# Sums of squares per token of a hybrid attention layer, taken from the columns of x in place of its rows

## The chip, the cores and the metric

The kernel runs on one core of a Trainium2 chip. The metric is the device time of one execution in microseconds. The engines are TensorE (PE, its weight loads are PEld), VectorE (DVE), ScalarE (ACT), GpSimd (POOL) and SyncE (SP), which here only issues loads and stores.

## What is computed

One decoder layer on x of 512 tokens by 1024, all float32. Cut to what matters here:

```python
u = rms_norm(h, attn_pre_g)                 # x * rsqrt(mean(x*x) + 1e-6) * g, by token
proj = u @ w_in                             # 1024 -> 256 + 128 + 32 + 3*512
c_q, c_kv, k_r, moba_qkv = split(proj)      # latents (256 and 128), rotary key, q/k/v of 8 heads
mla_o = mla_attention(rms_norm(c_q), rms_norm(c_kv), k_r, ...)
moba_o = moba_attention(rope(q), rope(k), v)
h = h + rms_norm(concat(mla_o, moba_o) @ w_out, attn_post_g)
h = h + rms_norm(square(relu(rms_norm(h, mlp_pre_g) @ w_up)) @ w_down, mlp_post_g)
```

The change is in the first norm. Its sum of squares over the 1024 elements of each token gives one root per token, `rstd = (mean + eps) ** -0.5`.

## The kernel before, in words

Every large product is made in three passes from two float32r parts of each operand (`mm3`, L1325): hi x hi, hi x lo, lo x hi. ScalarE makes the hi part (`hi_part`, L574), VectorE the lo part (`lo_part`, L879; `lo_scaled`, L882, with the gain).

x comes to the core twice at the start. Its columns, `x_cols` (transposed on the host, with the gain as a 513th column), are loaded in eight pieces of 128 x 513 into `x_raw` (`first_x`, L358) and become `uT_hi` and `uT_lo`, the operands of all projections. They are not normed: the roots of the tokens are multiplied in later. Its rows are loaded into `x_sb` (L373) only for the sums of squares. The weights `w_in` come in chunks: chunks 0 and 1 row by row with the columns (`first_rows`, L361), the others as 1 MB each (`chunk`, L335; `in_chunk`, L344) into two raw buffers in turn. Each load waits until VectorE is done with the chunk two before it (`w_ready`).

Order of work at the start, on each engine:

- TensorE: 34 small products to warm up, `first_group` (L1338) for latents and rotary key of four tiles of 128 tokens in banks 0 to 3, then `half_group(1, before_queries)` (L1377, L1395) for the queries in banks 4 to 7. This group has two parts of four chunks of rows each (`part`), a part has four tiles j of 12 products. Ahead of tile j=2 of part 0 it turns the four columns of token roots into a row in bank 7 (L1400); tile j=3 then uses bank 7, once VectorE has copied it to `r_cols`. The latents' transposes (L1425) and the key group `half_group(2, before_keys)` follow.
- ScalarE: hi parts of the eight pieces (`first_hi`), hi part of chunk 2 (`in_hi(2)`), four squares of x rows with `accum_out` into `stat` (`square`, L597; L616), hi part of chunk 3, then for each tile of 128 tokens the squares of both latents and a scaled copy of the rotary key (L620).
- VectorE: lo parts of the eight pieces (`first_lo`), lo part of chunk 2 (`in_lo(2)`, L915), the copy to `r_cols` (L917), lo part of chunk 3, rotation tables times roots (L922), normed latents `cn` (L930), rotation of the rotary key, lo part of chunk 4.
- GpSimd: constants, then `rms` (L484) once for each of the four tiles of tokens, and twice more for each tile for the latents. It takes the mean in one operation on a 128x1 column of `stat`, the power -0.5 in another and, for the latents, a product with the token's root in a third; each waits for the one before it. `stat[:, norm, tile, :]` holds sum (0), mean (2) and root (3) of a norm; norm 0 is the tokens', 1 and 2 are the latents'.

The order on each engine is the order of the code in its block; engines meet only at semaphores: `sq` counts sums of squares, `rstd` roots, `proj` finished projection tiles.

Of the kernel before, what the change touches and what calls it, by code (L numbers as in the profile page):

```python
# [20 lines left out]
ALU = mybir.AluOpType  # L21
ACT = mybir.ActivationFunctionType

P = 128
EPS = 1e-6
NEG = -1e30
NOPE, ROPE, VD = 64, 32, 64
# [5 lines left out]
def build(nc, x, attn_pre_g, w_in, mla_q_norm_g, w_mla_q_up, mla_kv_norm_g, w_mla_kv_up, w_out,  # L33
          attn_post_g, mlp_pre_g, w_up, w_down, mlp_post_g, rope_table, x_cols, rope_cols, out):
    S, D = x.shape[1], x.shape[2]
    F = w_up.shape[2]
    QR, KVR = w_mla_q_up.shape[1], w_mla_kv_up.shape[1]
    NT = S // P
    ND = D // P
# [9 lines left out]
    x_v = x[0].rearrange("(t p) d -> t p d", p=P)  # L49
# [26 lines left out]
    with ExitStack() as ctx:  # L76
        def sb(name, shape, dt=F32, stack=ctx):
            return stack.enter_context(nc.sbuf_tensor(name, shape, dt))

        def sem(name):  # L80
            return ctx.enter_context(nc.semaphore(name))
# [7 lines left out]
        stat = sb("stat", [P, 6, NT, 4])  # L89
        half = stat[:, 4, 0, 1:2]  # L90
        nb = sb("nb", [P, 4, NT])
# [26 lines left out]
        with ExitStack() as start:  # L118
            x_sb = sb("x_sb", [P, NT, D], stack=start)
            junk_pre = sb("junk_pre", [P, D], BF16, stack=start)  # L120
# [5 lines left out]
        with ExitStack() as pre:  # L126
            lat_g = sb("lat_g", [P, QR + KVR], stack=pre)
            rope_sb = sb("rope_sb", [P, NT, rope_table.shape[1]], stack=pre)
            cn = sb("cn", [P, NT, QR + KVR], stack=pre)
            kr = sb("kr", [P, NT, ROPE], stack=pre)  # L130
            krr = sb("krr", [P, NT, ROPE], stack=pre)
            r_cols = sb("r_cols", [P, S], stack=pre)
            turn = sb("turn", [P, 2, S], stack=pre)
            rt1 = sb("rt1", [P, NT, HW], stack=pre)
            rt2 = sb("rt2", [P, 2, HW], stack=pre)
# [35 lines left out]

        x_in = [sem(f"x{t}_in") for t in range(NT)]
        x_cols_in = [sem(f"x_cols{k}_in") for k in range(ND)]
# [13 lines left out]
        sq = sem("sq")  # L187
# [146 lines left out]
        def _(sp):  # L334
# [37 lines left out]
            in_chunk(2)  # L372
            for t in range(NT):  # L373
                sp.dma_start(x_sb[:, t, :], x_v[t]).then_inc(x_in[t], 16)
            sp.dma_start(rope_sb[:, :, :], rope_table.rearrange("(t p) c -> p t c", p=P)).then_inc(tab_in, 16)
            sp.dma_start(lat_g[:, 0:QR], mla_q_norm_g.to_broadcast([P, QR])).then_inc(lat_in, 16)
# [90 lines left out]
        def _(pool):  # L467
# [3 lines left out]
            nc.gpsimd.memset(half, -0.5).then_inc(zeroed, 1)  # L471
            pool.wait_ge(zeroed, 3)
            nc.gpsimd.affine_select(out=ident[:, :], in_=ident[:, :], compare_op=ALU.not_equal, fill=1.0, base=0,
# [25 lines left out]

            for t in range(NT):  # L500
                rms(0, t, D, t + 1)

            for t in range(NT):
                rms(1, t, QR, NT + 2 * t + 1, by=stat[:, 0, t, 3:4])
                rms(2, t, KVR, NT + 2 * t + 2, by=stat[:, 0, t, 3:4])

# [52 lines left out]
        def _(act):  # L559
# [34 lines left out]

            squares = [0]

            def square(src, norm, t, col, scale=1.0):  # L597
                if squares[0]:
                    act.wait_ge(sq, squares[0])
                squares[0] += 1  # L600
                junk = junk_pre if norm <= 2 else junk_post if norm <= 4 else junk_down
                nc.scalar.activation(junk[:, 0:src.shape[1]], src, ACT.Square, scale=scale,  # L602
                                     accum_out=stat[:, norm, t, col:col + 1]).then_inc(sq, 1)
# [11 lines left out]
            in_hi(2)  # L615
            for t in range(NT):  # L616
                act.wait_ge(x_in[t], 16)
                square(x_sb[:, t, :], 0, t, 0)
            in_hi(3)
# [251 lines left out]
        def _(dve):  # L871
# [41 lines left out]
            for k in range(ND):  # L913
                first_lo(k)
            in_lo(2)  # L915
            dve.wait_ge(r_full, 1)
            nc.vector.tensor_copy(r_cols[:, :], ps[7][:, :]).then_inc(r_ready, 1)  # L917
# [8 lines left out]
            for t in range(NT):  # L926
                dve.wait_ge(kr_c, t + 1)
                for norm, c0, n in ((1, 0, QR), (2, QR, KVR)):
                    dve.wait_ge(rstd, NT + 2 * t + norm)
                    nc.vector.scalar_tensor_tensor(out=cn[:, t, c0:c0 + n], in0=ps[t][:, c0:c0 + n],  # L930
                                                   scalar=stat[:, norm, t, 3:4], in1=lat_g[:, c0:c0 + n],
                                                   op0=ALU.mult, op1=ALU.mult).then_inc(cn_ready, 1)
# [391 lines left out]
        def _(pe):  # L1324
# [70 lines left out]
            def before_queries(part, j):  # L1395

                if part == 0 and j == 2:
                    pe.wait_ge(rstd, NT)
                    for t in range(NT):
                        last = nc.tensor.transpose(ps[7][:, P * t:P * t + P], stat[:, 0, t, 3:4].to_broadcast([P, P]),  # L1400
                                                   ident[:, :])
                    last.then_inc(r_full, 1)
                if part == 0 and j == 3:
                    pe.wait_ge(r_ready, 1)
# [366 lines left out]
```

## Time and profile before

| | us |
|---|---|
| median of 3 runs | 562.36 (562.35 to 562.46) |
| the profiled execution | 562.25 |
| its span, first to last instruction | 560.5 |
| TensorE busy | 548.9 (98%), 2730 instructions |
| VectorE busy | 392.2 (70%), 745 |
| ScalarE busy | 293.4 (52%), 612 |
| GpSimd busy | 92.2 (16%), 152 |
| moved by DMA | 99.66 MB |

All times below are from the start of the span, which is 1.75 us shorter than the execution. The trace writes the buffers of PSUM as `bank`, without their number, and names of buffers without their numbers. A product's record covers its way through the pipeline, so records overlap: the distance between two starts is what one costs in a row of them. "Idle before" is what an engine sat idle ahead of an instruction, with what ended it.

### The profile page before, as it was taken

The numbers are of one execution on the slowest core, as the hardware profiler recorded it, in microseconds if no ns is written. First come the engines' busy times: TensorE is split into PE (matmuls) and PEld (weight loads), VectorE is DVE, ScalarE is ACT, GpSimd is POOL, SyncE is SP. The second block draws the span as 40 slices with busy tenths as digits, with TensorE's granted clock in tenths as the row PEclk, the third lists the DMA queues.
The fourth block names the chain that finished last, engine by engine and source line by source line (L and its number), as shares of the span: only waits on it lengthen the run. The fifth ranks groups of instructions, "written<-read, shape, count | busy, mean of one in ns | idle before, by whom it ended". The sixth has DMA issues, their size and how long they took to land.

```text
span 560.5 us, 7840 instructions
## 1 busy us (share of the span) xinstructions
PE 548.9 (98%) x2730; PEld 451.9 (81%) x2730; DVE 392.2 (70%) x745; ACT 293.4 (52%) x612; POOL 92.2 (16%) x152
## 2 busy tenths in 40 slices
PE   9999999999999999999999999999999999999994
PEld 8888898876656888988888888888888888888883
DVE  5359473487785366367766775779777989778897
ACT  6563172688884364463344335344465656656561
POOL 1263110355784012200000000000000001000003
PEclk9999999999999999999999999999999999999999
DMA  8933652000002940387778886787975565605403
GB/s 289 370 123 104 201 165 76 0 2 2 0 2 76 340 149 1 108 297 272 229 277 279 278 283 229 276 279 265 357 280 195 181 216 167 219 21 204 150 1 150
DMA packets 43454, 99.66 MB, mean 178 GB/s; under 512 B 3232, under 2 KB 20896, under 8 KB 40096
## 3 DMA queue, kind: packets, MB, share of 16 engines
q1 hardware_dynamic: 42992, 98.54, 51.0%
q10 hardware_dynamic: 432, 0.74, 0.4%
q8 instruction: 17, 0.28, 0.2%
q14 instruction: 13, 0.11, 0.1%
HBM read 81.44 MB, written 15.73 MB: 173 GB/s over the span
## 4 chain that ended last, share of the span: by engine, by line
PE 91%; DMA 3%; DVE 2%; POOL 2%; ACT 1%; issue 1%; ACTq 0%; DVEq 0%; POOLq 0%
PE bank L1327 28%; PE bank L1328 27%; PE bank L1329 27%; PE bank L1539 3%; PE bank L1558 3%; POOL probs L527 1%; DMA w_raw<-in_w_in 1%; DMA x_raw<-in_x_cols 1%; PE bank L1504 1%; DVE w_lo L883 1%; PE bank L1333 1%; DVE bank L1000 1%; ACT w_hi L575 1%; ACT probs L665 0%; PE bank L1463 0%
## 5 line engine op out<-in xcount | busy, mean ns | idle before, releaser
L1327 PE MATMUL bank<-uT_hi,w_hi 128*128 128x512 f32 (+1 forms) x344 | 129.3, 376 | 0.8 <-DVE w_lo L883 0.8
L1328 PE MATMUL bank<-uT_lo,w_hi 128*128 128x512 f32 (+1 forms) x344 | 128.8, 374 | 0.0
L1329 PE MATMUL bank<-uT_hi,w_lo 128*128 128x512 f32 (+1 forms) x344 | 128.7, 374 | 0.0
L1327 PE MATMUL bank<-w_hi,a_hi 128*128 128x512 f32 x224 | 87.2, 389 | 0.0
L1329 PE MATMUL bank<-w_hi,a_lo 128*128 128x512 f32 x224 | 87.2, 389 | 0.0
L1328 PE MATMUL bank<-w_lo,a_hi 128*128 128x512 f32 x224 | 87.1, 389 | 0.0
L883 DVE SCALAR_TENSOR_TENSOR w_lo<-w_raw,g_up,w_hi 128x256 fp32r<-128x256 f32 x128 | 52.1, 480 | 48.4 <-ACT w_hi L575 48.4
L575 ACT ACTIVATE w_hi<-w_raw,g_up 128x256 fp32r<-128x256 f32 x128 | 53.0, 496 | 45.6 <-PE bank L1329 24.8
L1327 PEld LDWEIGHTS bank<-uT_hi,w_hi 128*128 128x128 f32 x344 | 64.7, 188 | 12.9 <-issue 1.1
L1328 PEld LDWEIGHTS bank<-uT_lo,w_hi 128*128 128x128 f32 x344 | 64.8, 188 | 11.5
L1329 PEld LDWEIGHTS bank<-uT_hi,w_lo 128*128 128x128 f32 x344 | 64.7, 188 | 11.4
L575 ACT ACTIVATE w_hi<-w_raw 128x1024 fp32r<-128x1024 f32 (+2 forms) x49 | 46.4, 996 | 52.4 <-PE bank L1329 48.8
L880 DVE TENSOR_TENSOR w_lo<-w_raw,w_hi 128x1024 fp32r<-128x1024 f32 (+2 forms) x45 | 51.4, 1185 | 21.5 <-ACT w_hi L575 21.5
L527 POOL TENSOR_TENSOR probs<-probs,rs 128x512 f32<-128x512 f32 (+3 forms) x64 | 44.1, 720 | 50.9 <-DVE rs L1020 44.9
L1327 PEld LDWEIGHTS bank<-w_hi,a_hi 128*128 128x128 f32 x224 | 42.0, 188 | 9.2 <-issue 0.4
L1329 PEld LDWEIGHTS bank<-w_hi,a_lo 128*128 128x128 f32 x224 | 42.0, 188 | 8.8
L1328 PEld LDWEIGHTS bank<-w_lo,a_hi 128*128 128x128 f32 x224 | 42.0, 188 | 8.6
L822 ACT ACTIVATE act_sb<-relu 128x512 f32 (+1 forms) x32 | 20.0, 624 | 51.1 <-DVE relu L1186 51.1
L551 POOL TENSOR_TENSOR relu<-relu,post_g 128x512 f32<-128x512 f32 x2 | 2.7, 1394 | 230.9 <-ACT junk_down L602 230.9
L665 ACT ACTIVATE probs<-bank,nb 128x512 f32<-128x512 f32 (+3 forms) x64 | 33.2, 524 | 13.9 <-DVE nb L1000 13.4
L1208 DVE TENSOR_TENSOR stage<-stage 128x512 f32<-128x512 f32 x56 | 38.7, 691 | 1.5
L1000 DVE CUSTOM_DVE_ANT_0 bank<-bank,mask 128x512 f32<-128x512 f32 (+3 forms) x64 | 30.0, 515 | 12.4 <-PE bank L1329 6.2
(161 smaller groups left out, 871.3 us busy)
## 6 DMA issues: line engine op xcount, KB each, us to landing
stage<-in_w_down SPq DMA_DIRECT2D x17, 1024.0 KB, 4.9
w_raw<-in_w_up SPq DMA_DIRECT2D x16, 1024.0 KB, 8.4
pair_sums<-stage SPq DMA_DIRECT2D x13, 1024.0 KB, 9.9
w_raw<-in_w_down SPq DMA_DIRECT2D x10, 1024.0 KB, 6.7
w_raw<-pair_sums SPq DMA_DIRECT2D x10, 1024.0 KB, 4.8
w_raw<-in_w_in SPq DMA_DIRECT2D x6, 1024.0 KB, 7.5
w_raw<-in_w_out SPq DMA_DIRECT2D x4, 1024.0 KB, 4.8
stage<-pair_sums SPq DMA_DIRECT2D x3, 1024.0 KB, 4.8
```

What stands on the lines that cost most here:

```text
L527: nc.gpsimd.tensor_tensor(pr, pr, rs[:, i % 4, t:t + 1].to_broadcast([P, P * (t + 1)]), ALU.mult).then_inc(s_norm, 1)
L575: return nc.scalar.activation(out, whole, ACT.Copy, scale=scale)
L665: nc.scalar.activation(probs[i % 4][:, p_off(t):p_off(t) + n], ps[b][:, c:c + n], ACT.Exp, bias=nb[:, i % 4, t:t + 1], scale=-1.0, accum_o ...
L822: nc.scalar.activation(act_sb[:, bass.ds(i * 4 + tile, 1), :], relu[:, tile % 2:tile % 2 + 1, :], ACT.Square).then_inc(a_ready, 1)
L880: return nc.vector.tensor_tensor(out, whole, hi.bitcast(F32), ALU.subtract)
L883: return nc.vector.scalar_tensor_tensor(out=out, in0=whole, scalar=scale, in1=hi.bitcast(F32), op0=ALU.mult, op1=ALU.subtract)
L1000: nc.vector.tensor_tensor_reduce(out=s, in0=s, in1=mask[:, TOP - P * (t + 1):], scale=-SCALE[i], scalar=-NEG, op0=ALU.add, op1=ALU.min, ac ...
L1208: nc.vector.tensor_tensor(total, a, b, ALU.subtract).then_inc(stage_sums, 1)
L1327: nc.tensor.matmul(out, lh, rh, start=start, stop=False)
L1328: nc.tensor.matmul(out, lh, rl, start=False, stop=False)
L1329: return nc.tensor.matmul(out, ll, rh, start=False, stop=stop)
L1539: last = nc.tensor.transpose(ps[b][:, c + P * (t - k):c + P * (t - k) + P], probs[i % 4][:, p_off(t) + P * k:p_off(t) + P * k + P], ident[ ...
```

## The change

It takes the sums of squares from `x_raw`, the columns, in place of `x_sb`, the rows:

- ScalarE squares the eight pieces of columns into `sq_cols` (8 x 128x512 float32) where it squared the four tiles of rows.
- VectorE adds the eight into the first, seven additions of 128x512, behind the lo part of chunk 2 and ahead of the copy to `r_cols`. Each waits for its square and for the addition before it.
- TensorE makes the sums over the 128 partitions: four plain float32 products with `sq_cols` as weights (128 x 128 each) and a column of ones, one column of bank 7 each, ahead of tile j=1 of part 0. It waits for the seventh addition.
- VectorE copies the four columns from bank 7 into `stat`, GpSimd makes the four roots in one pair of operations on 128x4.
- The latents' roots are made in six operations on 128x4 once all eight of their sums are there.
- The four loads of x rows at the start go; the rotation table comes in the layout of its buffer, so that each partition's part is one piece.

```diff
-        half = stat[:, 4, 0, 1:2]
+        half, one = stat[:, 4, 0, 1:2], stat[:, 4, 1, 1:2]
...
-            x_sb = sb("x_sb", [P, NT, D], stack=start)
+            sq_cols = sb("sq_cols", [P, ND, S], stack=start)
...
             in_chunk(2)
-            for t in range(NT):
-                sp.dma_start(x_sb[:, t, :], x_v[t]).then_inc(x_in[t], 16)
-            sp.dma_start(rope_sb[:, :, :], rope_table.rearrange("(t p) c -> p t c", p=P)).then_inc(tab_in, 16)
+            sp.dma_start(rope_sb[:, :, :], rope_table).then_inc(tab_in, 16)
...
-            for t in range(NT):
-                rms(0, t, D, t + 1)
-
-            for t in range(NT):
-                rms(1, t, QR, NT + 2 * t + 1, by=stat[:, 0, t, 3:4])
-                rms(2, t, KVR, NT + 2 * t + 2, by=stat[:, 0, t, 3:4])
+            pool.wait_ge(sq, NT)
+            step(nc.gpsimd.tensor_scalar(stat[:, 0, :, 2], stat[:, 0, :, 0], 1.0 / D, EPS, ALU.mult, ALU.add))
+            nc.gpsimd.tensor_tensor(stat[:, 0, :, 3], stat[:, 0, :, 2], half.to_broadcast([P, NT]), ALU.pow).then_inc(rstd, NT)
+
+            pool.wait_ge(sq, 3 * NT)
+            for norm, n in ((1, QR), (2, KVR)):
+                last = nc.gpsimd.tensor_scalar(stat[:, norm, :, 2], stat[:, norm, :, 0], 1.0 / n, EPS, ALU.mult, ALU.add)
+            step(last)
+            for norm in (1, 2):
+                last = nc.gpsimd.tensor_tensor(stat[:, norm, :, 3], stat[:, norm, :, 2], half.to_broadcast([P, NT]), ALU.pow)
+            step(last)
+            for norm in (1, 2):
+                nc.gpsimd.tensor_tensor(stat[:, norm, :, 3], stat[:, norm, :, 3], stat[:, 0, :, 3],
+                                        ALU.mult).then_inc(rstd, NT)
...
             in_hi(2)
-            for t in range(NT):
-                act.wait_ge(x_in[t], 16)
-                square(x_sb[:, t, :], 0, t, 0)
+            for k in range(ND):
+                nc.scalar.activation(sq_cols[:, k, :], x_raw[:, k, 0:S], ACT.Square).then_inc(x_squared, 1)
             in_hi(3)
...
             in_lo(2)
+            for k in range(1, ND):
+                dve.wait_ge(x_squared, k + 1)
+                if k >= 2:
+                    dve.wait_ge(x_summed, k - 1)
+                nc.vector.tensor_tensor(sq_cols[:, 0, :], sq_cols[:, 0, :], sq_cols[:, k, :], ALU.add).then_inc(x_summed, 1)
+            dve.wait_ge(x_sums, 1)
+            nc.vector.tensor_copy(stat[:, 0, :, 0], ps[7][:, 0:NT]).then_inc(sq, NT)
             dve.wait_ge(r_full, 1)
...
-                    dve.wait_ge(rstd, NT + 2 * t + norm)
+                    dve.wait_ge(rstd, NT + NT * norm)
...
             def before_queries(part, j):
 
+                if part == 0 and j == 1:
+                    pe.wait_ge(x_summed, ND - 1)
+                    for t in range(NT):
+                        last = nc.tensor.matmul(ps[7][:, t:t + 1], sq_cols[:, 0, P * t:P * t + P], one, start=True, stop=True)
+                    last.then_inc(x_sums, 1)
                 if part == 0 and j == 2:
```

TensorE, from the end of tile j=0 to the root transposes, before (L1327 to L1329 are the three passes of `mm3`, L1400 the transposes):

```order
L1327 MATMUL bank<-uT_hi,w_hi 128x512
L1328 MATMUL bank<-uT_lo,w_hi 128x512
L1329 MATMUL bank<-uT_hi,w_lo 128x512
L1400 MATMUL bank<-ident,stat 128x128 [waits rstd]
L1400 MATMUL bank<-ident,stat 128x128 x3
```

Ahead of these stand the 24 products of j=0 and j=1 without a wait but the first one's. And with the change (L1339 to L1341 are now the three passes, L1417 the transposes), from the last products of j=0 to the first of j=1:

```order
L1339 MATMUL bank<-uT_hi,w_hi 128x512
L1340 MATMUL bank<-uT_lo,w_hi 128x512
L1341 MATMUL bank<-uT_hi,w_lo 128x512
L1412 MATMUL bank<-stat,sq_cols 128x1 [waits x_summed]
L1412 MATMUL bank<-stat,sq_cols 128x1 x3
L1339 MATMUL bank<-uT_hi,w_hi 128x512
L1340 MATMUL bank<-uT_lo,w_hi 128x512
L1341 MATMUL bank<-uT_hi,w_lo 128x512
```

A wait and four products now stand between j=0 and j=1; the transposes keep their place behind j=1.

VectorE, around the lo part of chunk 2, before:

```order
L883 SCALAR_TENSOR_TENSOR w_lo<-w_raw,g_in,w_hi 128x512 [waits wh_ready]
L883 SCALAR_TENSOR_TENSOR w_lo<-w_raw,g_in,w_hi 128x512 x3
L917 COPY r_cols<-bank 128x512 [waits r_full]
L883 SCALAR_TENSOR_TENSOR w_lo<-w_raw,g_in,w_hi 128x512 [waits wh_ready]
L883 SCALAR_TENSOR_TENSOR w_lo<-w_raw,g_in,w_hi 128x512 x3
```

and with the change:

```order
L888 SCALAR_TENSOR_TENSOR w_lo<-w_raw,g_in,w_hi 128x512 [waits wh_ready]
L888 SCALAR_TENSOR_TENSOR w_lo<-w_raw,g_in,w_hi 128x512 x3
L925 TENSOR_TENSOR sq_cols<-sq_cols 128x512 [waits x_squared]
L925 TENSOR_TENSOR sq_cols<-sq_cols 128x512 [waits x_summed,x_squared] x6
L927 COPY stat<-bank 128x4 [waits x_sums]
L929 COPY r_cols<-bank 128x512 [waits r_full]
```

Seven additions and a copy that waits for TensorE stand between the lo part of chunk 2 and `r_cols`.

## Rows read from the trace of the kernel before

**Rows 1.** The profile's chain that ended last, shares of the span by engine.
```profile
PE 91%; DMA 3%; DVE 2%; POOL 2%; ACT 1%; issue 1%; ACTq 0%; DVEq 0%; POOLq 0%
```
**Rows 2.** Waits of TensorE, 0 to 250 us: in total, times, longest.
```profile
PE bank L1327 <- DVE w_lo L883: 0.8, 1, 0.8
```
**Rows 3.** The chain in order of time, 0 to 60 us: start, us, what.
```profile
10.95 7.80 DMA w_raw<-in_w_in
18.83 2.57 ACT w_hi L575 x4
21.43 2.75 DVE w_lo L883 x4
```
**Rows 4.** Timeline, TensorE: start, us, instruction, [idle before <-releaser].
```profile
24.31 0.47 PE L1327 MATMUL bank<-uT_hi,w_hi 128*128 128x512 f32 x1 [0.79 <-DVE w_lo L883]
...
27.13 0.39 PE L1327 MATMUL bank<-uT_hi,w_hi 128*128 128x512 f32 x1
...
29.85 0.60 PE L1400 MATMUL bank<-ident,stat 128*128 128x128 f32 x4
...
46.66 1.48 PE L1425 MATMUL bank<-ident,cn 128*128 128x128 f32 x12
47.97 0.60 PE L1429 MATMUL bank<-ident,krr 128*32 128x128 f32 x4
```
**Rows 5.** Timeline, ScalarE.
```profile
11.28 0.63 ACT L575 ACTIVATE uT_hi<-x_raw 128x512 fp32r<-128x512 f32 x1
...
21.30 1.04 ACT L602 ACTIVATE junk_pre<-x_sb 128x1024 bf16<-128x1024 f32 x1
...
30.14 0.45 ACT L602 ACTIVATE junk_pre<-bank,stat 128x256 bf16<-128x256 f32 x1
```
**Rows 6.** Timeline, issues of DMA by SyncE (SPq).
```profile
11.38 3.40 SPq L374 DMA_DIRECT2D x_sb<-in_x  x4
...
232.54 0.37 SPq L399 DMA_DIRECT2D stage<-in_w_down  x1
232.95 0.47 SPq L407 DMA_DIRECT2D w_raw<-in_w_up  x1
```
**Rows 7.** Timeline, GpSimd.
```profile
22.97 0.94 POOL L494 TENSOR_TENSOR stat<-stat 128x1 f32<-128x1 f32 x1
...
41.95 0.19 POOL L497 TENSOR_TENSOR stat<-stat 128x1 f32<-128x1 f32 x1
...
66.55 2.54 POOL L510 TENSOR_TENSOR rt<-rt 128x512 f32<-128x512 f32 x2 [13.86 <-DVE rt L958]
```
**Rows 8.** Issues at 10.95, 232.54, 232.95: count, KB, us to landing.
```profile
w_raw<-in_w_in SPq DMA_DIRECT2D x1, 1024.0 KB, 7.8
...
stage<-in_w_down SPq DMA_DIRECT2D x1, 1024.0 KB, 4.9
...
w_raw<-in_w_up SPq DMA_DIRECT2D x1, 1024.0 KB, 7.5
```
**Rows 9.** Timeline, VectorE.
```profile
4.40 0.44 DVE L899 TENSOR_SCALAR w_hi<-w_raw,x_raw 128x416 fp32r<-128x416 f32 x1 [4.40 <-DMA x_raw<-in_x_cols]
4.87 0.65 DVE L883 SCALAR_TENSOR_TENSOR w_lo<-w_raw,x_raw,w_hi 128x416 fp32r<-128x416 f32 x1
...
15.51 0.68 DVE L880 TENSOR_TENSOR uT_lo<-x_raw,uT_hi 128x512 fp32r<-128x512 f32 x1
...
42.64 0.22 DVE L944 TENSOR_TENSOR rt<-kr,rope_sb 128x64 f32<-128x64 f32 x1
```
**Rows 10.** Groups by shape, TensorE, 110 to 190 us: count | busy, mean ns.
```profile
L1504 PE MATMUL bank<-mkT,mqT 64*128 64x512 f32 x16 | 4.5, 641 | 0.6 <-ACT probs L665 0.6
...
L1504 PE MATMUL bank<-mkT,mqT 64*128 64x128 f32 x16 | 1.6, 270 | 0.0
```
**Rows 11.** Windows: us, busy of PE, PEld, DVE, ACT, POOL, clock, DMA share, GB/s.
```profile
553.00:555.00 2.00, 0.10 (x1) 0.00 (x0) 1.83 (x3) 0.72 (x2) 0.98 (x3) 1.00 0.00 0
...
557.00:559.00 2.00, 0.00 (x0) 0.00 (x0) 1.01 (x2) 0.00 (x0) 0.00 (x0) 0.77 0.62 238
```

More of the change, by code:

```diff
@@ L127, in build @@
             lat_g = sb("lat_g", [P, QR + KVR], stack=pre)
-            rope_sb = sb("rope_sb", [P, NT, rope_table.shape[1]], stack=pre)
+            rope_sb = sb("rope_sb", [P, NT, rope_table.shape[2]], stack=pre)
             cn = sb("cn", [P, NT, QR + KVR], stack=pre)
@@ L169, in build @@
         ps = [ctx.enter_context(nc.psum_tensor(f"bank{b}", [P, TOP], F32)) for b in range(8)]
-        x_in = [sem(f"x{t}_in") for t in range(NT)]
+        x_squared, x_summed, x_sums = sem("x_squared"), sem("x_summed"), sem("x_sums")
         x_cols_in = [sem(f"x_cols{k}_in") for k in range(ND)]
@@ L471, in _ @@
             nc.gpsimd.memset(half, -0.5).then_inc(zeroed, 1)
-            pool.wait_ge(zeroed, 3)
+            nc.gpsimd.memset(one, 1.0).then_inc(zeroed, 1)
+            pool.wait_ge(zeroed, 4)
             nc.gpsimd.affine_select(out=ident[:, :], in_=ident[:, :], compare_op=ALU.not_equal, fill=1.0, base=0,
@@ L593, in first_hi @@
                     hi_part(w_hi[w_slot(k // 4)][:, w], raw[k // 4][:, w], g_first(k)).then_inc(in_rows(k, first_h, wh_ready)[0], 1)
-            squares = [0]
+            squares = [NT]
             def square(src, norm, t, col, scale=1.0):
-                if squares[0]:
-                    act.wait_ge(sq, squares[0])
+                act.wait_ge(sq, squares[0])
                 squares[0] += 1
@@ L1757 @@
     arrays = {name: np.ascontiguousarray(inputs[name]) for name in NAMES}
-    arrays["rope_table"] = rope_constants(arrays["x"].shape[1], ROPE, 1)
+    table = rope_constants(arrays["x"].shape[1], ROPE, 1)
+    arrays["rope_table"] = np.ascontiguousarray(table.reshape(-1, P, table.shape[1]).transpose(1, 0, 2))
     arrays["x_cols"] = np.ascontiguousarray(np.concatenate([arrays["x"][0].T, arrays["attn_pre_g"][0][:, None]], axis=1))
```

## The prediction

> **What bounds the kernel now.** I read four views in this order. The chain that ended last [rows 1] puts 91% of the span on TensorE. So a change at the start is worth what it does to TensorE's instruction stream: a microsecond that another engine saves or spends there counts only if TensorE waits for it, and no later stage of the kernel waits for a load that could take a delay back.
>
> The list of waits for the first 250 us [rows 2] has one wait of TensorE between its first projection product and the attention: 0.8 us for `w_lo` of the first query chunk (chunk 2). The chain in order of time [rows 3] shows what lies behind it: the load of that chunk is issued at 10.95 and lands 7.80 us later, ScalarE makes `w_hi` from 18.83 (2.57), VectorE makes `w_lo` from 21.43 (2.75), and TensorE starts at 24.31. TensorE's own rows [rows 4] then give the timetable that the change has to fit: tile j=0 of the query group runs from 24.31 to 27.13, j=1 follows without a gap, and the four transposes of the token roots stand at 29.85, where nothing is waited for. So the only thing to gain is under 0.8 us, and everything else in this stretch is cover that can be used up.
>
> **Removed work.** ScalarE loses four squares over rows of x, 1.04 us and an accumulator read each [rows 5]; the four loads of x rows (2 MB) go, with 3.40 us of SP's issue time [rows 6]. None of it lies on the path: ScalarE's row squares start after `w_hi` of chunk 2, which is what TensorE waits for. GpSimd's roots shrink from 8 to 2 instructions for the tokens and from 24 to 6 for the latents. The last of the 24 ends at 42.14 [rows 7] while TensorE needs the latents only at 46.66 [rows 4], so this was covered by more than 3 us and is worth nothing, too. The table of rotations in another layout and the one extra constant cost nothing: the table is wanted long after it lands, and the constant is set before anything waits for GpSimd again.
>
> **Does chunk 2 land earlier without the x rows?** They are issued directly behind it [rows 6], and it takes 7.8 us where a 1 MB load from an idle queue takes 4.9 [rows 8], so they could be to blame. The nearest row says no: the load issued at 232.54 [rows 6] landed after 4.9 us although the next 1 MB load was issued 0.41 us behind it at 232.95; that second one took 7.5, as long as one that stands in line. Loads of this queue are served in line. Chunk 2 is late for what stands ahead of it, the first rows of w_in and the columns of x, which the change leaves alone. I take no gain; the bounds are none and 7.8 - 4.9 = 2.9 us.
> The Trainium skill, *DMA: Bandwidth & Descriptors*, section "Queues, rings and completion order", has the same rule: each DMA engine consumes a queue's descriptors in ring order. It speaks against the change, which takes away only loads that stand behind; these rows agree with it.
>
> **The new chain in front of j=1.** This is the term that matters. VectorE's seven adds stand behind `w_lo` of chunk 2 in its order and need each other's result. `w_lo` is done at 21.43 + 2.75 = 24.18 [rows 3]. An operation of two 128x512 fp32 tensors takes 0.68, the third row of [rows 9]; one that waits for the instruction before it on its own engine starts 0.03 after that one's end (4.40 + 0.44 = 4.84 against 4.87, the first two rows there). So 7 x 0.71 = 5.0 us, to 29.18. ScalarE's eight squares don't hold them up: they start at 21.4, and at 0.63 each [rows 5] even laid end to end they are through at 26.4, when the last add is not due before 28.4. TensorE gets the word 0.13 us after VectorE's end (24.18 to 24.31), so its products can start at 29.31. The change has it wait for them ahead of j=1, which started at 27.13: **a stall of 2.2 us** where there was none. Nothing covers it, because TensorE is in order and the 36 products of j=1 to 3, though ready, are queued behind the wait.
>
> **The four products.** One column each, plain fp32. The trace has 16 records of 64x512 scores products [rows 10] for 8 in the program (four pairs of heads, two heads), so a plain fp32 product is two loads of weights and two passes: eight here. The twelve transposes at 46.66, also short and with a load each, take 1.31 to the next instruction at 47.97: 0.109 each [rows 4]. Eight make **0.87 us**. Below: four at that price, 0.44, should each be one pass. Above: eight at the 0.27 that a whole short product lasts, the last row of [rows 10], 2.2. I take the middle row because its conditions, loads that nothing long hides, are nearest.
>
> **What is late next.** The token roots now begin after the products: VectorE's copy of 128x4 (under the 0.22 of 128x64 [rows 9]), two GpSimd operations, the power 0.94 [rows 7] and a shorter one (at most as much again), and three hand-overs of 0.1: at most 2.4 us, beside j=1's 2.7, so TensorE doesn't wait at the root transposes. The latents' squares on ScalarE, which start at 30.14 now [rows 5], then start 2.2 to 3 us later, for want of the roots. From there to the last of the latents' roots it is 12.0 us now (42.14), and there are 18 GpSimd operations fewer in it; even if it took as long, it would end at 45.1 where TensorE has moved from 46.66 to 49.7. Covered as before.
>
> **Sum**: 2.19 + 0.87 = +3.06 us. The profiled execution took 562.25, so 565.3; the median of the runs shown stands 0.11 above that execution, which I leave aside. What a measurement of this kernel can tell from no change is about 0.2%, 1.1 us; the forecast, slower, lies beyond it.
>
> **Rivals.**
> *Chunk 2 comes early* (the other side). If the x rows did take its bandwidth, it could land up to 2.9 us earlier, at 15.85. The adds would end at 26.4, TensorE would start j=0 at 23.52 instead of 24.31 (the 0.79 of [rows 4] gone) and be through at 26.34; the products run from 26.4 to 27.3, 0.15 later than j=1 before: 562.4, not slower. Each 1 us of earlier landing takes 1 us off; from 1.95 us on the result is within 0.2%. For it: 7.8 against 4.9. Against it: the pair at 232.54. If the products also cost only 0.44, it ends 0.3 us faster, still not by 0.2%.
> *The wait moves on to the roots.* If GpSimd's power over four columns costs four times that over one, 3.8 us instead of 0.94 [rows 7], the chain behind the products is at most 5.2 us against 2.7 of cover: up to 2.5 more, 565.3 to 567.8. It decides from a power of 1.25 us on. For it: the power is dear for a single column. Against it: tensor operations of that engine over 512 columns take 1.27 (two in 2.54 at 66.55 [rows 7]), so a further column of a multiplication costs next to nothing.
>
> *The clock falls.* TensorE would idle for 2.2 us and then do almost nothing for 0.9, and if its clock fell to the lower of its two levels (1.2 GHz), the next tile would take 2.7 us more, 568. Against it: in the tail TensorE has 0.10 us of work left after 553, and the granted clock is still 1.00 until 555 and has a mean of 0.77 from 557 to 559 [rows 11]. The Trainium skill, *TensorE: Matmul & The Clock Gate*, section "What's actually happening", says that an idle array is put to 1.2 GHz; this trace agrees, but the fall comes some 4 us or more after the last product, and the gap here would be 3.1.
> *The change doesn't do what it says*: x rows are still loaded, but only later for the residual; in this stretch they are gone. I give this nothing.
>
> **How the numbers follow.** The forecast's own case 0.80: with the products between 0.44 and 2.2, and up to half a microsecond of earlier landing, 562.25 + 2.1 to 562.25 + 4.4. Early landing 0.09, of which most within 0.2%, some above it. Roots 0.08, clock 0.02, anything that is faster by more than 0.2% 0.01. The range 563.7 to 566.7 takes in the first case, the upper end of early landing and half of the roots' case. Faster 0.01, within 0.2% 0.08, slower 0.91.
>
> **What would show it.** Right: TensorE's first gap of 0.8 us in place, a second of about 2.2 ahead of the four products with the seventh add as its releaser, eight short records of some 0.9 in all, no gap ahead of the root transposes, chunk 2 landing about 7.8 us after its issue, and all that follows moved by 3 us. Wrong: a landing before 17.5; a gap ahead of the transposes with GpSimd as its releaser; matmuls of 128x512 at twice their spacing behind the gap; adds spaced by other than 0.71.

## The result, and the profile after

The changed kernel takes 566.96 us, median of six runs (564.78 to 569.12), against 562.36 for the one before (562.06 to 562.47): a ratio of 1.0082, 95% interval 1.0066 to 1.0097. It is slower, as forecast, but by 4.6 us where 3.1 were forecast, and the median lies outside the range of 563.7 to 566.7. The execution that was profiled is the fastest of the six, 564.78 us, and for it the sum of the prediction (565.3) was right to 0.5 us. Each execution has a mean granted clock of TensorE (1 is 2.4 GHz): 0.998 in the profiled one, 0.990 to 0.995 in the other five. So the question is what the other five did. Its page:

```profile
span 563.0 us, 7843 instructions
PE 549.7 (98%) x2738; PEld 452.7 (80%) x2738; DVE 396.2 (70%) x753; ACT 293.0 (52%) x612; POOL 84.2 (15%) x129
```

TensorE's waits up to 45 us, and its timeline around the new products. (L1339 to L1341 are the three passes of a projection product, L1412 the new products, L1417 the root transposes, L925 the additions.)

```profile
PE bank L1412 <- DVE sq_cols L925: 2.3, 1, 2.3
...
PE bank L1339 <- DVE w_lo L888: 0.5, 1, 0.5
```
```profile
23.87 0.47 PE L1339 MATMUL bank<-uT_hi,w_hi 128*128 128x512 f32 x1 [0.52 <-DVE w_lo L888]
26.45 0.39 PE L1341 MATMUL bank<-uT_hi,w_lo 128*128 128x512 f32 x1
29.16 1.05 PE L1412 MATMUL bank<-stat,sq_cols 128*128 128x1 f32 x8 [2.32 <-DVE sq_cols L925]
30.07 0.48 PE L1339 MATMUL bank<-uT_hi,w_hi 128*128 128x512 f32 x1
32.90 0.60 PE L1417 MATMUL bank<-ident,stat 128*128 128x128 f32 x4
```

Against [rows 4]: the first gap is 0.52 instead of 0.79, a second one of 2.32 stands ahead of eight records of one column, these take 0.91 to the next product (29.16 to 30.07), and nothing is waited for at the transposes, which come 3.05 later than at 29.85. At the last product of the kernel 2.84 of that is left (555.55 against 552.71), and what follows it is 0.3 shorter in this execution. VectorE and GpSimd beside it:

```profile
20.98 2.74 DVE L888 SCALAR_TENSOR_TENSOR w_lo<-w_raw,g_in,w_hi 128x512 fp32r<-128x512 f32 x4 [4.86 <-ACT w_hi L582]
23.64 5.46 DVE L925 TENSOR_TENSOR sq_cols<-sq_cols 128x512 f32<-128x512 f32 x7
```
```profile
30.57 0.20 POOL L500 TENSOR_SCALAR stat<-stat 128x4 f32<-128x4 f32 x1 [28.18 <-DVE stat L927]
30.93 1.04 POOL L501 TENSOR_TENSOR stat<-stat 128x4 f32<-128x4 f32 x1 [0.15 <-POOL stat L500]
```

The seven additions take 5.46 us, 0.795 from one start to the next, and the power over four columns costs 1.04 where one column cost 0.94 in the row of [rows 7] (ten of the kernel's twelve powers over one column took 0.55 or 0.56).

### The profile page after: what moved, and what is told of

It reads as the page before. It is cut to its first block, busy times and chain, and to the rows that moved or that the text cites. A ratio compares the mean times of both kernels' runs of the same rounds, so it can differ in the third digit from the quotient of the medians.

```text
span 563.0 us, 7843 instructions
## 1 busy us (share of the span) xinstructions
PE 549.7 (98%) x2738; PEld 452.7 (80%) x2738; DVE 396.2 (70%) x753; ACT 293.0 (52%) x612; POOL 84.2 (15%) x129
## 4 chain that ended last, share of the span: by engine, by line
PE 91%; DVE 3%; DMA 2%; ACT 1%; POOL 1%; issue 1%; ACTq 0%; POOLq 0%; DVEq 0%
PE bank L1339 28%; PE bank L1340 27%; PE bank L1341 27%; PE bank L1556 3%; PE bank L1575 3%; DMA w_raw<-in_w_in 1%; DMA x_raw<-in_x_cols 1%; POOL probs L534 1%; DVE sq_cols L925 1%; PE bank L1521 1%; DVE w_lo L888 1%; PE bank L1345 1%; ACT w_hi L582 1%; PE bank L1480 1%; ACT probs L670 0%
## 5 line engine op out<-in xcount | busy, mean ns | idle before, releaser
L1339 PE MATMUL bank<-uT_hi,w_hi 128*128 128x512 f32 (+1 forms) x344 | 129.3, 376 | 0.5 <-DVE w_lo L888 0.5
L1341 PE MATMUL bank<-uT_hi,w_lo 128*128 128x512 f32 (+1 forms) x344 | 128.8, 374 | 0.0
L1339 PE MATMUL bank<-w_hi,a_hi 128*128 128x512 f32 x224 | 87.2, 389 | 0.0
L1341 PE MATMUL bank<-w_hi,a_lo 128*128 128x512 f32 x224 | 87.1, 389 | 0.0
L1339 PEld LDWEIGHTS bank<-uT_hi,w_hi 128*128 128x128 f32 x344 | 64.7, 188 | 12.4 <-issue 0.8
L1341 PEld LDWEIGHTS bank<-uT_hi,w_lo 128*128 128x128 f32 x344 | 64.7, 188 | 11.4
L582 ACT ACTIVATE w_hi<-w_raw 128x1024 fp32r<-128x1024 f32 (+2 forms) x49 | 46.4, 996 | 52.0 <-PE bank L1341 48.5
L1339 PEld LDWEIGHTS bank<-w_hi,a_hi 128*128 128x128 f32 x224 | 42.0, 188 | 9.1 <-issue 0.4
L1341 PEld LDWEIGHTS bank<-w_hi,a_lo 128*128 128x128 f32 x224 | 42.0, 188 | 8.8
```

Source lines behind the costliest of these rows:

```text
L582: return nc.scalar.activation(out, whole, ACT.Copy, scale=scale)
L1339: nc.tensor.matmul(out, lh, rh, start=start, stop=False)
L1341: return nc.tensor.matmul(out, ll, rh, start=False, stop=stop)
```

## The experiments

Twelve runs, in groups that shared a chip and its runs of the kernel before (medians 562.54, 562.26 and 562.22).

### The changed kernel again, with a profile (again)

> The changed kernel itself, once more. Theory A (the clock): the gap of TensorE of 2.3 us and the 1.05 us of one-column products behind it let the chip grant a lower clock for a while in most executions, but not in all, as it depends on where in time the gap falls: single executions between 564.7 and 569, their mean granted clock 0.998 in the fast ones and 0.990 to 0.995 in the others, and a profile of a slow one shows matmuls of 128x512 at twice their spacing of 0.23 somewhere from 29 us on, with the granted clock at half there. Theory B (a load): the landing of chunk 2, or another load, varies from run to run now; then the granted clock stays at 0.998 in all of them and the profile of a slow one shows a longer gap instead.

566.77 us (564.40 to 568.01), ratio 1.007 (1.0052 to 1.0087). This time the profile caught an execution with the loss (567.23, mean clock 0.992). TensorE's timeline, then its windows of one microsecond (busy time of PE, PEld, DVE, ACT, POOL; then the granted clock):

```profile
29.80 1.05 PE L1412 MATMUL bank<-stat,sq_cols 128*128 128x1 f32 x8 [2.29 <-DVE sq_cols L925]
...
31.79 0.63 PE L1339 MATMUL bank<-uT_hi,w_hi 128*128 128x512 f32 x1
32.21 0.63 PE L1340 MATMUL bank<-uT_lo,w_hi 128*128 128x512 f32 x1
```
```profile
30.00:31.00 1.00, 1.00 (x9) 0.99 (x9) 0.04 (x1) 0.00 (x0) 0.00 (x0) 1.00 0.00 0
31.00:32.00 1.00, 1.00 (x4) 0.77 (x3) 0.12 (x1) 0.00 (x0) 0.64 (x2) 0.56 0.00 0
32.00:33.00 1.00, 1.00 (x3) 0.78 (x3) 0.00 (x0) 0.36 (x1) 0.60 (x1) 0.50 0.00 0
33.00:34.00 1.00, 1.00 (x4) 0.74 (x3) 0.00 (x0) 0.97 (x6) 0.00 (x0) 0.50 0.00 0
34.00:35.00 1.00, 1.00 (x5) 0.82 (x4) 0.00 (x0) 0.97 (x6) 0.00 (x0) 0.73 0.00 0
35.00:36.00 1.00, 1.00 (x8) 0.86 (x7) 0.23 (x1) 0.97 (x6) 0.00 (x0) 1.00 0.00 0
```

The clock falls to the lower of its two levels (0.50 of full speed, 1.2 GHz). It does so not in the gap, which runs from 27.51 to 29.80, but behind it, in the middle of the products of j=1: these now follow each other every 0.42 us instead of 0.23. By the windows it is at half from about 31.1 to 34.5, 3.4 us, in which half of the work is lost: 1.7 us. From the start of j=0 to the start of the key group it is 29.08 us here (24.51 to 53.59) and 27.51 in the first profile of the same kernel (23.87 to 51.38): 1.6 us. The profiled execution of the first run shows 1.00 in all these windows.

### The gap filled with 36 small products (fill)

```diff
                 if part == 0 and j == 1:
+                    for _ in range(36):
+                        nc.tensor.matmul(ps[7][:, 0:P], warm_b[:, :], warm_b[:, :], start=True, stop=True)
                     pe.wait_ge(x_summed, ND - 1)
```

> The changed kernel with 36 small bf16 products (128x128, the ones of the warm-up, some 0.056 us each at the full clock, 2.0 us in all) in TensorE's gap ahead of the wait for the last addition; nothing reads them. Theory A (the clock): the engine stays active, the clock stays up, and every execution takes 564.5 to 565.2, within 0.3 of each other. Theory B (a load varies): the same spread as the changed kernel's, 564.7 to 569, with a median near 567.

564.83 us (564.65 to 564.96), ratio 1.0041 (1.0028 to 1.0054), mean clock 0.995 to 0.998 in all executions. The timeline:

```profile
26.50 2.18 PE L1411 MATMUL bank<-warm_b 128*128 128x128 bf16 x36
...
28.94 1.05 PE L1414 MATMUL bank<-stat,sq_cols 128*128 128x1 f32 x8 [0.26 <-DVE sq_cols L925]
```

TensorE gets no result earlier, it is only kept at work, and the kernel is 566.77 - 564.83 = 1.94 us faster. That is what keeping the clock up is worth at the median; the traces put 1.6 us on the one fall that was profiled (29.08 in again against 27.50 here, from j=0 to the keys). Where the rest of the 1.94 lies isn't shown: the two medians come from six and five executions, and again's profile also starts j=0 later by 0.85.

### Half as many small products (fill_half)

The same with `range(18)`.

> As fill, with 18 small products in place of 36: TensorE works 1.1 us longer after j=0 and then sits idle for 1.2 to 1.3 us before the one-column products. If it is the idle stretch as a whole that brings the clock down, half of it is short enough and every execution takes 564.6 to 565; if the light stretch (one-column products) counts as idle too, or the fall depends on little, some executions show a clock under 0.998 and the median is above 565.3.

564.75 us (563.73 to 566.16), ratio 1.0048 (1.0034 to 1.0062). A gap of 1.30 was left. One of six executions had the low mean clock (566.16 us, 0.993), the others 0.996 to 0.998. So the fall seems rarer behind a shorter gap, but not impossible. The 564.6 to 565 that was expected of every execution, should half the idle stretch be short enough, did not hold; nor did the median above 565.3 of the other case.

### The kernel before with a wait alone (stall)

```diff
+                if part == 0 and j == 1:
+                    pe.wait_ge(wh_ready, 4)
```

> The kernel before with a wait alone: ahead of tile j=1 TensorE waits until ScalarE has the hi part of chunk 3, which it had at 30.2 us; a gap of 3.1 us, no new work on any engine. Theory A (the clock): the wait costs its own 3.1 us in some executions (565.4) and up to 4 more in others, with a granted clock under 0.998 in those; median over 566. Theory B (the loads of the changed kernel vary, not the clock): 565.3 to 565.6 in all executions.

566.96 us (564.89 to 567.30), ratio 1.0073 (1.006 to 1.0087). In its profile TensorE waits 3.86 us, and the clock is 0.89 in the window 31 to 32 and 0.50 in the next:

```profile
30.44 0.50 PE L1327 MATMUL bank<-uT_hi,w_hi 128*128 128x512 f32 x1 [3.86 <-ACT w_hi L575]
```
```profile
31.00:32.00 1.00, 1.00 (x5) 0.82 (x4) 0.00 (x0) 1.00 (x5) 0.84 (x3) 0.89 0.02 8
32.00:33.00 1.00, 1.00 (x4) 0.75 (x3) 0.00 (x0) 0.97 (x6) 0.75 (x4) 0.50 0.00 0
```

The gap is longer than the changed kernel's, so its time says nothing of the 2.3 us. But without one new product or addition the clock falls: a gap alone is enough, and the one-column products aren't needed for it. Whether they add to it behind the shorter gap of the changed kernel isn't shown. Here again one execution of six kept its clock (0.998).

### Squares and additions ahead of chunk 2 (early)

```diff
+            square_cols(0, 6)
             in_hi(2)
-            for k in range(ND):
-                nc.scalar.activation(sq_cols[:, k, :], x_raw[:, k, 0:S], ACT.Square).then_inc(x_squared, 1)
+            square_cols(6, ND)
...
+            add_cols(1, 6)
             in_lo(2)
...
+            add_cols(6, ND)
```

(The two helpers hold the loops of the change, with its waits.)

> The changed kernel with the first six squares ahead of the hi part of chunk 2 on ScalarE, which sits idle for 3.6 us there, and five of the seven additions ahead of its lo part on VectorE (idle 4.9 us). The last addition then ends near 25.3, before j=0 is through at 26.7: no gap ahead of the products. Both theories: 562.25 + 0.9 for the products - 0.3 for the earlier landing = 562.9, in all executions within 0.3, as the gap is gone; if ScalarE's squares delay the hi part by 0.2, 563.1. If it takes 564 or more, the gap was not what cost the 2.3 us.

562.58 us (561.96 to 562.92), ratio 1.0 (0.9991 to 1.0009). Six squares and five additions go where both engines wait for the load of chunk 2; two additions are left behind `w_lo`. VectorE's and TensorE's timelines:

```profile
16.21 3.87 DVE L929 TENSOR_TENSOR sq_cols<-sq_cols 128x512 f32<-128x512 f32 x5
```
```profile
23.98 0.47 PE L1347 MATMUL bank<-uT_hi,w_hi 128*128 128x512 f32 x1 [0.33 <-DVE w_lo L892]
...
26.81 0.94 PE L1420 MATMUL bank<-stat,sq_cols 128*128 128x1 f32 x8
27.62 0.49 PE L1347 MATMUL bank<-uT_hi,w_hi 128*128 128x512 f32 x1
```

The gap is gone, the products cost 0.81, and `w_lo` isn't late. This version computes the same as the changed kernel and is 4.2 us faster: 2.25 of stall (fill less early) and 1.94 of clock (again less fill).

### The last squares on GpSimd (pool_help)

```diff
+            for k in (6, 7):
+                pool.wait_ge(x_cols_in[k], 16)
+                nc.gpsimd.tensor_tensor(sq_cols[:, k, :], x_raw[:, k, 0:S], x_raw[:, k, 0:S], ALU.mult).then_inc(x_pool, 1)
+            pool.wait_ge(x_pool, 2)
+            nc.gpsimd.tensor_tensor(sq_cols[:, 6, :], sq_cols[:, 6, :], sq_cols[:, 7, :], ALU.add).then_inc(x_pool, 1)
...
-                if part == 0 and j == 1:
-                    pe.wait_ge(x_summed, ND - 1)
+                if part == 0 and j == 0:
+                    pe.wait_ge(x_summed, ND - 2)
```

> As early, with the last two squares and their sum on GpSimd, which is idle there (three operations of 128x512, 1.27 each), six additions on VectorE all ahead of the lo part of chunk 2, and the four products ahead of tile j=0, where TensorE waits for that lo part anyway. Early took 562.58. The products then cost what sticks out of the gap of 0.3 to 0.6 us, 0.3 to 0.6 instead of 0.8: 562.1 to 562.4, the same as before within 0.2%. If GpSimd is slowed beside VectorE so that its sum comes after 20.9, VectorE's last addition delays the lo part, and it is 562.6 to 563.5.

(The diff is against early. All six squares left on ScalarE and all six additions left on VectorE, one fewer than in early, stand ahead of chunk 2's parts.) 563.71 us (563.45 to 565.62), ratio 1.0034 (1.0021 to 1.0047): a miss. VectorE's timeline while GpSimd squared and added (12.3 to 16.4), and behind it; then GpSimd's:

```profile
11.59 0.68 DVE L895 TENSOR_TENSOR uT_lo<-x_raw,uT_hi 128x512 fp32r<-128x512 f32 x1
12.29 1.50 DVE L898 SCALAR_TENSOR_TENSOR w_lo<-w_raw,x_raw,w_hi 128x416 fp32r<-128x416 f32 x1
13.71 1.52 DVE L895 TENSOR_TENSOR uT_lo<-x_raw,uT_hi 128x512 fp32r<-128x512 f32 x1
15.16 1.69 DVE L898 SCALAR_TENSOR_TENSOR w_lo<-w_raw,x_raw,w_hi 128x416 fp32r<-128x416 f32 x1
16.77 0.68 DVE L895 TENSOR_TENSOR uT_lo<-x_raw,uT_hi 128x512 fp32r<-128x512 f32 x1
```
```profile
12.30 2.39 POOL L502 TENSOR_TENSOR sq_cols<-x_raw 128x512 f32<-128x512 f32 x2 [9.90 <-DMA x_raw<-in_x_cols]
14.77 1.63 POOL L504 TENSOR_TENSOR sq_cols<-sq_cols 128x512 f32<-128x512 f32 x1
```

VectorE's operations took over twice as long beside GpSimd's, 1.52 against 0.68 for the same lo part. GpSimd's sum wasn't late (16.40, where the expectation named 20.9); VectorE's own queue was, and TensorE waited 1.54 us ahead of j=0. Behind that gap, too, one execution of six has a low mean clock (565.62 us, 0.993).

### The kernel before without the loads of x rows (no_rows)

```diff
-            for t in range(NT):
-                sp.dma_start(x_sb[:, t, :], x_v[t]).then_inc(x_in[t], 16)
...
-                square(x_sb[:, t, :], 0, t, 0)
+                square(x_raw[:, 2 * t:2 * t + 2, 0:S], 0, t, 0)
```

> The kernel before without its four loads of x rows at the start; the four squares read two pieces of x_raw each instead (1024 elements, the same durations), so the roots are of other numbers and the output is not the layer's. Theory 1 (loads are served in line): chunk 2 lands 7.4 to 7.8 us after its issue as before, the time is 562.0 to 562.5, within 0.2% of before. Theory 2 (the rows took its bandwidth): it lands after 5 to 6 us, TensorE's gap of 0.8 us is gone and the time is 561.6 to 561.8.

561.20 us (560.72 to 561.37), ratio 0.9982 (0.9974 to 0.9991): 1.06 us under the kernel before, more than either theory allowed, though chunk 2 landed as late as ever (7.6 us behind its issue, as in before_twice with the rows). This raised a question that the next three runs answer.

### The latents' roots four at once, alone (roots, roots_twice)

```diff
-            for t in range(NT):
-                rms(1, t, QR, NT + 2 * t + 1, by=stat[:, 0, t, 3:4])
-                rms(2, t, KVR, NT + 2 * t + 2, by=stat[:, 0, t, 3:4])
+            pool.wait_ge(sq, 3 * NT)
+            for norm, n in ((1, QR), (2, KVR)):
+                last = nc.gpsimd.tensor_scalar(stat[:, norm, :, 2], stat[:, norm, :, 0], 1.0 / n, EPS, ALU.mult, ALU.add)
...
```

(The powers and the products by the tokens' roots follow in the same manner, and VectorE's waits are set to match.)

> The kernel before with the latents' roots alone made four tiles at once, as in the change. They end before 42 as before, TensorE needs them at 46.7: no difference, 562.2 to 562.6. If batching them delays the first tile's so much that the lo part of chunk 4 and the rotations end after 48.5, TensorE waits ahead of the keys and it is 0.3 to 1 us slower.

> Latents' roots four tiles at once, alone, a second time beside the kernel before on one chip. If the gain of 0.14% in the first run was the edit, the median is again 0.8 to 1.0 us under the one of the kernel before (561.2 to 561.5). If it was variation, the two lie within 0.4 us of each other.

561.30 us (560.81 to 562.92), ratio 0.9986 (0.9977 to 0.9994), and again 561.21 us (560.45 to 563.34), ratio 0.9984 (0.9975 to 0.9992). The edit is worth 1.0 us, twice, and its profiled TensorE started j=0 at 23.56 in one execution and at 24.28 in the other.

### The kernel before, profiled once more (before_twice)

> The kernel before, once more, profiled in its own right, to see how far its own executions and its stall in front of the first w_lo product vary. If the 1.0 us that the runs without the rows and with the roots alone gained is variation of the executions and not of the edits: a median of 562.3 here with single executions from 561.3 to 562.8, and a stall in front of w_lo anywhere from 0 to 0.8 us. If it is the edits: 562.2 to 562.5 with a stall near 0.8 us, and no profile without a stall.

562.29 us (561.83 to 562.85). The profile shows a stall that the first one hadn't. TensorE's timeline at the end of the first query part; GpSimd's and VectorE's just before:

```profile
23.60 0.47 PE L1327 MATMUL bank<-uT_hi,w_hi 128*128 128x512 f32 x1 [0.33 <-DVE w_lo L883]
...
45.97 1.48 PE L1425 MATMUL bank<-ident,cn 128*128 128x128 f32 x12
47.28 0.60 PE L1429 MATMUL bank<-ident,krr 128*32 128x128 f32 x4
48.97 0.50 PE L1327 MATMUL bank<-uT_hi,w_hi 128*128 128x512 f32 x1 [1.08 <-DVE rt L958]
```
```profile
42.36 0.19 POOL L497 TENSOR_TENSOR stat<-stat 128x1 f32<-128x1 f32 x1
```
```profile
42.59 0.35 DVE L930 SCALAR_TENSOR_TENSOR cn<-bank,stat,lat_g 128x128 f32<-128x128 f32 x1 [0.63 <-POOL stat L497]
...
43.77 2.74 DVE L883 SCALAR_TENSOR_TENSOR w_lo<-w_raw,g_in,w_hi 128x512 fp32r<-128x512 f32 x4
...
48.23 0.68 DVE L958 TENSOR_TENSOR rt<-bank,turn 128x512 f32<-128x512 f32 x1
```

VectorE takes a latent as soon as its root is there, but behind the last one stand the key's rotation, the lo part of chunk 4 and four operations of the query rotations (L957, L958), and TensorE's key group needs the banks that these free. From the last root to the last of these (42.55 to 48.91) nothing is idle. So in the kernel before, TensorE's stream past 48.5 was set by GpSimd's 24 root operations, whether or not TensorE came early to j=0. (One of them, a mean over a single column, lasted 1.78 us here instead of 0.19, from 32.82 to 34.60, while VectorE multiplied two tensors of 128x512, L922, from 33.27 to 34.56. How much of the wait is due to that wasn't tested.) In the first profile the gap ahead of j=0 had been 0.79, TensorE came late enough, and 48.55 fell just on the end of the rotation: the wait was there, but had a length of nothing.

Both single edits take this wait away. With the roots alone the last root operation ends at 39.02 (roots) and 37.94 (roots_twice), and no wait for VectorE is seen. The executions profiled in before_twice and roots both came early to j=0 (23.60 and 23.56), and the key group starts at 48.97 in one and in the other at:

```profile
47.70 0.50 PE L1334 MATMUL bank<-uT_hi,w_hi 128*128 128x512 f32 x1
```

That is 1.27 us, and it stays: from this start to the last product of the kernel it is 504.1 to 504.2 us in every trace kept, 504.4 in no_rows. Without the rows it is chunk 3 that comes earlier, whose hi part stands ahead of the latents' squares on ScalarE. Its landing, by the DMA views of the kernel before and of no_rows (issued at 17.12 and at 15.32):

```profile
w_raw<-in_w_in SPq DMA_DIRECT2D x1, 1024.0 KB, 10.5
```
```profile
w_raw<-in_w_in SPq DMA_DIRECT2D x1, 1024.0 KB, 6.0
```

27.6 against 21.3, of which 1.8 us is the earlier issue and 4.5 the shorter way from issue to landing. The two edits together were not run by themselves; as both remove the same wait, their gains should not add. Early, which has both, fits: with 0.81 us of products it is level with the kernel before, so it gained some 0.8 and not 2.

### One addition instead of seven (one_add)

```diff
-            for k in range(1, ND):
+            for k in range(1, 2):
...
-                    pe.wait_ge(x_summed, ND - 1)
+                    pe.wait_ge(x_summed, 1)
```

> The changed kernel with one addition of the seven, so that its sum takes only two columns in (six additions are left out); the order of the engines is otherwise the changed one. The additions' chain of 7 x 0.795 us shrinks to one, which ends at about 24.4 us, before TensorE has ended the product with u_hi and w_lo of the first output (26.9 us): no stall, so no fall of the clock. Theory (the chain makes the stall, the stall the fall): the kernel before's time plus the 0.8 to 1.0 us of the four products, 562.3 to 563.4. Rival (something else in the changed code costs, as the squares on ScalarE that delay chunk 3, or the wait itself): 565 or more.

561.87 us (561.54 to 562.65), ratio 0.9995 (0.9986 to 1.0004). No gap ahead of the products, no fall (the clock is 1.00 from 26 to 38), and 5 us less than the changed kernel with everything else in place:

```profile
26.59 0.39 PE L1341 MATMUL bank<-uT_hi,w_lo 128*128 128x512 f32 x1
26.82 0.94 PE L1412 MATMUL bank<-stat,sq_cols 128*128 128x1 f32 x8
27.63 0.49 PE L1339 MATMUL bank<-uT_hi,w_hi 128*128 128x512 f32 x1
```

It came out under the expected 562.3, 0.35 below its kernel before: the microsecond that the roots give back (-1.0) and the products (+0.8) account for -0.2 of it, and the rest is within the interval.

### Early with the products issued twice (early_double)

> The version with the squares and additions ahead of chunk 2's w_hi and w_lo, with the four one-column products issued twice (the second four into columns that nobody reads). The second four cost 0.8 to 1.0 us more on TensorE, by 8 x 0.1 us: 563.3 to 563.6, against 562.6 for the version with four. If the products are hidden beside other work, as the latents' or the early gain, 562.6 again. If eight make the clock fall, 566.

563.29 us (562.83 to 564.12), ratio 1.0023 (1.0014 to 1.0032): 1.07 us over its kernel before, where early is 0.04 over its own. The rows:

```profile
26.86 0.95 PE L1420 MATMUL bank<-stat,sq_cols 128*128 128x1 f32 x8
27.67 1.03 PE L1422 MATMUL bank<-stat,sq_cols 128*128 128x1 f32 x8
28.56 0.49 PE L1347 MATMUL bank<-uT_hi,w_hi 128*128 128x512 f32 x1
```

The first eight cost 0.81, the second 0.89. The products are paid in full, and nothing hides them.

## Why the prediction was wrong

With the runs of the first chip the difference of 4.23 us (566.77 to 562.54) splits: early less before 0.04, which is +0.81 of products and, as what is left over, about -0.8 of the wait behind the roots; fill less early 2.25, the stall; again less fill 1.94, the clock. The prediction had the stall and the products, gave the clock nothing in its sum and took the wait behind the roots for nothing.

- **The step that failed** is the rival *The clock falls*, held at 2 in 100. Its mechanism, its place and nearly its size (2.7 on top, 1.94 measured) were there; its argument against was wrong. From the tail [rows 11] I read that the fall comes some 4 us or more behind the last product (by windows of one microsecond it is 5.0, from 553.1 to 558.1), and concluded that a gap of 3.1 is too short. But the lag doesn't protect. In again the last full product ended at 27.51, and the clock fell at about 31.1, in the middle of products that had started again. What the tail showed was how late the fall comes, not how long a gap must be. The Trainium skill, *TensorE: Matmul & The Clock Gate*, "What's actually happening", has an idle array put to 1.2 GHz; the traces agree, and add that the array may by then no longer be idle.
- It isn't sure either: the same kernel, with gaps of 2.32 and 2.29, kept its clock in one execution and lost it in another. Of its twelve executions eight have a mean clock of 0.990 to 0.993 and take 566.3 us or more, two have 0.995 (565.94 and 566.48; a mean of 0.995 also occurs without a gap, as at 561.90 in before_twice, so the mean alone doesn't prove a fall), and the two with 0.998 take 564.40 and 564.78. What decides in a single execution stays open, and so does the slowest, 569.12: it is 4.3 over fill, more than one fall of 3.4 us takes, and has no profile.
- **The stall** of 2.2 was right within 0.3 us: counted as in the prediction, from where j=1 could have started (there 27.13 to 29.31, 2.18), it is 2.5 in the profile (26.68 to 29.16; the 2.32 of the row counts only from the end of the last record), 2.25 by the times. The chain of additions was sized too small: each comes 0.795 behind the one before it, not 0.71, and the seven take 5.46 instead of 5.0. That the products still started at 29.16, near the forecast 29.31, was luck: `w_lo` was done 0.5 us earlier in the profiled execution. The 0.03 between dependent instructions came from the row at 4.40, of another operation; it wasn't a row of this chain.
- **The products**: 0.87 forecast, 0.91 (changed kernel), 0.81 (early) and 0.89 (the second set of early_double) measured. Doubling them shows that they are on the path.
- **Chunk 2** landed after 7.5 us instead of 7.8. It was right that loads behind it don't delay it. What I left out is the load behind the rows, chunk 3. It stood in line behind them, and without them comes 6.3 us earlier (27.6 and 21.3). The ring order that the Trainium skill states in *DMA: Bandwidth & Descriptors*, "Queues, rings and completion order", speaks for this just as it spoke against chunk 2; the 10.5 and 6.0 us agree.
- **"Covered by more than 3 us and worth nothing"**, said of the latents' roots, was wrong by 1.0 us. I measured the cover to the transposes at 46.66, the first reader of the latents, and not along VectorE's queue behind them, whose last rotation ended with TensorE's start at 48.55. The views showed no wait there because its length was zero in that execution. How much it is depends on when TensorE comes to j=0: 0.25 in the pair that came late (24.31 and 24.28; the keys start at 48.55 before and at 48.30 in roots_twice), 1.27 in the pair that came early (23.60 and 23.56; 48.97 in before_twice, 47.70 in roots), 1.0 at the median of all executions. It worked against the clock: with it the forecast would have been lower, and the miss larger.
- **The roots' rival** fell: the power over four columns takes 1.04, under the 1.25 from which it would have decided, and no gap stands at the transposes.

## What to carry to other kernels

A new gap on TensorE can cost more than its length: look for the clock in the microseconds behind it, when work has resumed, and take several executions, since one profile may show none of it. Put work that needs each other's result where its engine waits anyway. And measure cover along the whole queue behind a step, to where another engine waits for that queue, not to the first reader; a wait of length zero is in no list.

The best of the versions is the kernel before with only the latents' roots changed, 561.21 and 561.30 us, 0.15% faster. Of those that sum over columns, early is level with the kernel before.

## What the runs showed of the hardware

- The clock fell behind gaps of 2.29 us (again) and 3.86 us (stall), started to fall at about 3.6 and 5.2 us behind the last full product, and stayed at 1.2 GHz for 3.4 us in again; behind gaps of 1.30 (fill_half) and 1.54 us (pool_help) one execution of six has a low mean clock; with 36 small bf16 products in the gap it stayed at 2.4 GHz in the profile, and all five executions lie within 0.3 us.
- GpSimd at work on 128x512 tensors slowed VectorE's operations from 0.68 to 1.52 us (pool_help), and a GpSimd operation on one column took 1.78 us instead of 0.19 beside two of VectorE's on 128x512 (before_twice).
- Dependent additions of 128x512 on VectorE follow each other every 0.795 us; two independent operations on tensors of this size in SBUF 0.61 (L922 of the kernel before, at 33.75: two in 1.29, the last of them 0.68).
- A power of GpSimd costs 0.55 us for one column (ten of the twelve in the kernel before; 0.94 in two) and 1.00 to 1.04 for four (early, the changed kernel): four columns in one instruction cost less than half of four instructions.
